# Differential attention with half of each combination on GpSimd and the turn and value product one unit later, together with six rearrangements at the joints between stages

## What is computed

```python
xn = rms_norm(x, norm_g[i]); proj = xn @ w_in[i]       # qa, ka, va, za, qb, kb, vb, zb
p1 = softmax(q1 @ k1.T * scale + t5_bias)              # differential attention, 4 heads,
p2 = softmax(q2 @ k2.T * scale + t5_bias)              # two maps of 64-wide queries and keys
oa = (p1 - lam * p2) @ va                              # values are 128 wide
ya = rms_norm(oa, subln_g[i]) * (1 - lam_init) * silu(za)
yb = neighbourhood_attention(qb, kb, vb, na_rpb[i]) * silu(zb)   # 8 heads, 8x16 windows
x = x + concat(ya, yb) @ w_out[i]
x = x + sigmoid(x @ w_ple_gate[i]) * (p[i] @ w_ple_proj[i])
```

## Time and profile before

| | us |
|---|---|
| median of 3 runs | 4010.92 |
| lowest and highest | 4009.79 to 4011.53 |
| the profiled execution | 4008.27 |
| its span, first to last instruction | 4006.5 |
| TensorE busy in the span | 3812.5 (95%) |
| VectorE, GpSimd, ScalarE busy | 2121.4, 1614.5, 1531.8 |
| mean granted TensorE clock | 0.985 |

### The profile page before, as it was taken

How to read it: one execution, slowest core, us unless ns; L and a number is a source line. 1 busy time by engine, 2 the same in 40 slices (tenths; PEclk the granted TensorE clock), 3 DMA queues, 4 the chain that set the end, 5 groups by cost and what they waited for, 6 DMA issues and landing times.

```text
span 4006.5 us, 52715 instructions
## 1 busy us (share of the span) xinstructions
PE 3812.5 (95%) x19336; PEld 3185.0 (79%) x19336; DVE 2121.4 (53%) x3622; ACT 1531.8 (38%) x2780; POOL 1614.5 (40%) x1394
## 2 busy tenths in 40 slices
PE   7999989889998999999999999897999999999999
PEld 6888777777876888778888888786888787888887
DVE  4553778523665767644454433765767643333233
ACT  4221667532334766622212122433766622222221
POOL 4242247342663610145544444563610135444442
PEclk9999999999999999999999999998999999999999
DMA  6775846320356422123233211356322131111111
GB/s 197 244 187 148 194 114 142 102 105 30 130 147 174 100 64 55 37 109 105 87 103 103 87 58 37 123 136 184 95 71 64 35 111 58 43 53 51 45 44 56
DMA packets 286153, 403.37 MB, mean 101 GB/s; under 512 B 43941, under 2 KB 206885, under 8 KB 285349
## 3 DMA queue, kind: packets, MB, share of 16 engines
q1 hardware_dynamic: 278984, 374.84, 32.7%
q10 hardware_dynamic: 6912, 25.17, 2.2%
HBM read 312.65 MB, written 96.45 MB: 102 GB/s over the span
## 4 chain that ended last, share of the span: by engine, by line
PE 71%; issue 10%; DVE 6%; POOL 5%; POOLq 2%; ACT 2%; DVEq 2%; DMA 1%; SPq 0%; ACTq 0%
PE ps L2638 6%; PE ps L2640 6%; PE ps L2639 6%; PE ps L2656 5%; PE ps L524 5%; PE ps L526 5%; PE ps L525 5%; PE ps L2658 5%; PE ps L2657 5%; PE ps L2059 3%; POOL rs L938 2%; PE ps L1705 2%; PE ps L1695 2%; PE ps L1696 2%; POOL WL L471 2%
## 5 line engine op out<-in xcount | busy, mean ns | idle before, releaser
L471 POOL TENSOR_TENSOR WL<-RAW,WH 128x1024 fp32r<-128x1024 f32 x225 | 555.5, 2480 | 752.3 <-ACT WH L445 742.2
L524 PE MATMUL ps<-WH,XTh 128*128 128x512 f32 (+1 forms) x1536 | 614.5, 400 | 38.5 <-POOL WL L471 13.6
L526 PE MATMUL ps<-WL,XTh 128*128 128x512 f32 (+1 forms) x1536 | 601.4, 392 | 0.0
L525 PE MATMUL ps<-WH,XTl 128*128 128x512 f32 (+1 forms) x1536 | 600.8, 391 | 0.0
L445 ACT ACTIVATE WH<-RAW 128x1024 fp32r<-128x1024 f32 x225 | 233.7, 1057 | 764.0 <-PE ps L2658 355.4
L2678 DVE TENSOR_TENSOR X<-ps,X 128x512 f32<-128x512 f32 x512 | 349.2, 689 | 249.5 <-PE ps L2658 248.3
L2656 PE MATMUL ps<-WH,Hh 128*128 128x512 f32 x1024 | 401.8, 392 | 4.2 <-DVE X L2678 3.9
L2669 DVE TENSOR_TENSOR MT<-ps,MT 128x512 f32<-128x512 f32 x128 | 88.5, 692 | 596.2 <-ACT MT L2692 591.2
L2638 PE MATMUL ps<-XTh,WH 128*128 128x512 f32 x1024 | 400.4, 391 | 2.3 <-ACT XTh L640 0.9
L2658 PE MATMUL ps<-WL,Hh 128*128 128x512 f32 x1024 | 399.0, 390 | 0.0
L2657 PE MATMUL ps<-WH,Hl 128*128 128x512 f32 x1024 | 398.9, 390 | 0.0
(11 more groups left out here) (274 smaller groups left out, 7770.4 us busy)
## 6 DMA issues: line engine op xcount, KB each, us to landing
RAW<-w_all SPq DMA_DIRECT2D x231, 512.0 KB, 3.6
WM<-w_mod ACTq DMA_DIRECT2D x48, 512.0 KB, 4.6
WM<-w_mod SPq DMA_DIRECT2D x48, 512.0 KB, 3.9
QKd<-KA_d SPq DMA_DIRECT2D x64, 256.0 KB, 5.8
QKm<-QM_d SPq DMA_DIRECT2D x32, 384.0 KB, 4.4
HEADK<-KA_d SPq DMA_DIRECT2D x32, 256.0 KB, 6.3
X_d<-X SPq DMA_DIRECT2D x2, 4096.0 KB, 12.6
QKd<-QA_d SPq DMA_DIRECT2D x16, 512.0 KB, 3.6
```

The source lines that it names most:

```text
L471: e.tensor_tensor(w_low(n), w_raw(n), w_high(n).bitcast(F32), ALU.subtract).then_inc(w_ready, 1)
L524: e.matmul(bank, a, w, start=(kc == 0), stop=False)
L525: e.matmul(bank, b, w, start=False, stop=False)
L526: j = e.matmul(bank, a, l, start=False, stop=(kc == K - 1))
```

## The change

In the differential attention, VectorE combines columns 0 to 511 and GpSimd columns 512 to 1023, in two operations: it scales the second map in place by the factor, then adds the first. The turn, the value product, the squares, copies, roots and output of a unit come one iteration later on their engines. TensorE's turn waits for GpSimd's part (`comb2`) after four transposes, and ScalarE's exponentials wait for it too. The loads of a head wait for the output instead of `used`, which is gone with its drain.

The six moves at joints: (1) the barrier ahead of the neighbourhood attention is gone; its first scores, maxima, exponential and three bias sums are issued inside the last iterations of the differential attention, Pn and BIn lie elsewhere, TensorE waits for the last output before it writes bank 7, and the memsets and first low values come at unit 5. (2) The PLE loads have two buffers (GT and G2) and stand, with the gate's first three weight pieces, ahead of the distance stores. (3) In the gate two squares come earlier, the highs come before the last tile's tanh and the lows in the loop. (4) The roots of the second half come between the projection's second and third weight piece. (5) A pair of "mkv" tiles shares one buffer and one store; there are three such buffers and one for "v". (6) In the dilated attention value_high(0) comes at u = 3 and the first low values at u = 4.

```diff
@@ -279,6 +278,7 @@
         c3.close()
+        PR = (GT[:], G2[:].rearrange("p a b -> p (a b)"))
         c3 = ExitStack()
...
@@ -546,7 +547,8 @@
                 if who.key == "pool":
-                    nm.roots(e, 1)
+                    if L != 1:
+                        nm.roots(e, 1)
                     if scaled(first + 3):
...
@@ -981,7 +997,7 @@
                 for k in pj.normed.get(n - 1, ()):
-                    if k in pj.vz:
+                    if k in pj.vz and pj.kinds[pj.tiles[k][0]]["half"] == 1:
                         v_store(k)
...
@@ -1083,13 +1099,13 @@
             diff_attention(who)
-            barrier(who)
             na_attention(who)
...
             distance_tables(who)
-            ple_load(who)
+            if key != "sp":
+                ple_load(who)
             gate_start(who)
...
@@ -1099,8 +1115,12 @@
                 if L == 0:
-                    if key in ("sp", "act", "pool"):
+                    if key in ("sp", "act"):
                         early(who, first, 1)
+                    if key == "pool":
+                        early(who, first, 1, 2)
+                        norm_of(1).roots(e, 1)
+                        early(who, first, 2)
                 turned = nt(who, NORM, 1 + 2 * L, X, True, first, led=norm_of(1 + 2 * L))
...
@@ -1438,9 +1458,9 @@
                     e.wait_ge(*rest_of_head(h - 1))
-                    e.wait_ge(s["used"], a.c(0) + h - 1)
+                    e.wait_ge(s["out"], a.c((h - 1) * T))
                     loads(h)
-                e.wait_ge(s["used"], a.c(0) + H_DIFF - 1)
+                e.wait_ge(s["out"], a.c((H_DIFF - 1) * T))
                 following = Heads("na", 0, 0)
...
@@ -1461,6 +1481,8 @@
                     for k in range(T):
+                        if k == T // 2:
+                            e.wait_ge(s["comb2"], a.c(u + 1))
                         j = e.transpose(ps[:, 4 + k // 4, (k % 4) * P:(k % 4) * P + P], BI[:, u % 2, k * P:k * P + P], ident[:])
...
@@ -1478,16 +1500,17 @@
                     scores(w)
-                for u in range(N + 1):
+                for u in range(N + 2):
                     if u + 2 < N:
...
                         scores(2 * u + 5)
-                    if u == N - 1:
-                        turn(u)
-                    if u >= 1:
-                        pv(u - 1)
-                    if u < N - 1:
-                        turn(u)
+                    if u == N + 1:
+                        e.wait_ge(s["max"], cm(2 * N))
+                        band_pe(who, Heads("na", 0, 0), "lead")
+                    if u >= 2:
+                        pv(u - 2)
+                    if 1 <= u <= N:
+                        turn(u - 1)
             if key == "dve":
...
@@ -1508,16 +1531,14 @@
                     e.drain()
-                    e.scalar_tensor_tensor(BI[:, u % 2, :], Pb[:, o + 1, :], li[:, u % 2:u % 2 + 1], Pb[:, o, :], ALU.mult,
-                                           ALU.add).then_inc(s["comb"], 1)
+                    e.scalar_tensor_tensor(BI[:, u % 2, 0:512], Pb[:, o + 1, 0:512], li[:, u % 2:u % 2 + 1], Pb[:, o, 0:512],
+                                           ALU.mult, ALU.add).then_inc(s["comb"], 1)
...
                                            ZS[:, home(h), t, :], ALU.mult, ALU.mult).then_inc(s["out"], 1)
-                    if t == T - 1:
-                        e.drain().then_inc(s["used"], 1)
...
@@ -1525,19 +1546,22 @@
                     e.wait_ge(v_stored(PJ["pj1"], i), 16 * T)
-                for u in range(N + 2):
+                for u in range(N + 3):
                     if u + 1 < N:
...
                         comb(u)
-                    if u >= 2:
-                        output(u - 2)
+                    if u == N + 2:
+                        band_dve(who, Heads("na", 0, 0), "lead")
+                    if u >= 3:
+                        output(u - 3)
             if key == "act":
...
                     e.wait_ge(s["comb"], a.c(u - 1))
+                    e.wait_ge(s["comb2"], a.c(u - 1))
                     o = 2 * (u % 2) + m
...
@@ -1558,16 +1582,27 @@
                 exps(1)
-                for u in range(N + 1):
+                for u in range(N + 2):
                     if u + 1 < N:
...
                         exps(2 * u + 3)
-                    if u >= 1:
-                        squares(u - 1)
-                    if u < N:
-                        copies(u)
+                    if u == N + 1:
+                        band_act(who, Heads("na", 0, 0), True)
+                    if u >= 2:
+                        squares(u - 2)
+                    if 1 <= u <= N:
+                        copies(u - 1)
             if key == "pool":
-                for u in range(N):
+                rest = slice(512, S)
+
+                def comb2(u):
+                    o = 2 * (u % 2)
+                    e.wait_ge(s["comb"], a.c(u + 1))
+                    e.tensor_scalar(Pb[:, o + 1, rest], Pb[:, o + 1, rest], li[:, u % 2:u % 2 + 1], None, ALU.mult)
+                    e.drain()
+                    e.tensor_tensor(BI[:, u % 2, rest], Pb[:, o + 1, rest], Pb[:, o, rest], ALU.add).then_inc(s["comb2"], 1)
+
+                def roots(u):
                     h, t = divmod(u, T)
...
@@ -1586,6 +1621,15 @@
+                for u in range(N + 2):
+                    if u < N:
+                        comb2(u)
+                    if u >= N:
+                        na_bias(e, u - N)
+                    if u >= 2:
+                        roots(u - 2)
+                na_bias(e, 2)
+
         def ge(e, s, value):
...
@@ -1758,10 +1802,12 @@
                     e.wait_ge(a.after.s["lo"], (a.after.L + 1) * a.after.ntr)
+                if u == 0 and a.kind == "na":
+                    e.wait_ge(AT["diff"]["out"], H_DIFF * T + CREDIT)
                 if u < N_UNITS:
...
-        def band_act(who, a):
+        def band_act(who, a, lead=False):
             e, s = who.e, a.s
...
@@ -1800,7 +1846,11 @@
-            exps(0)
+            if lead:
+                exps(0)
+                return
+            if a.kind == "dil":
+                exps(0)
             for u in range(N_UNITS + 6):
...
@@ -1808,12 +1858,12 @@
                     copy_out(u // 4 - 2)
-                if u == 1:
+                if u == (1 if a.kind == "na" else 3):
                     value_high(0)
...
-        def band_dve(who, a, part="all"):
+        def band_dve(who, a, part):
             e, s = who.e, a.s
...
@@ -1900,23 +1950,31 @@
+        def na_bias(e, u):
+            a = Heads("na", 0, 0)
+            h, t = divmod(u, T)
+            if u == 0:
+                e.wait_ge(a.s["pos"], 16)
+                e.wait_ge(*a.loaded(0))
+            e0 = (NA_START[t] - 2 * t + 8) * GRID_W
+            e.tensor_tensor(BIn[:, u % 3, :], NAB[:, h % 2, e0:e0 + NA_KEYS], RMK[:, NA_KIND[t], :], ALU.add).then_inc(a.s["bias"], 1)
+
         def na_pool(who, a):
...
                 h, t = divmod(u, T)
-                if u == 3:
+                if u == 5:
                     for t2 in range(T):
...
                     value_low(e, a, 0)
-                if t == 0:
+                if t == 0 and h:
                     e.wait_ge(*a.loaded(h))
...
                     e.wait_ge(s["max"], a.u0 + u - 2)
-                e0 = (NA_START[t] - 2 * t + 8) * GRID_W
-                e.tensor_tensor(BIn[:, u % 3, :], NAB[:, h % 2, e0:e0 + NA_KEYS], RMK[:, NA_KIND[t], :], ALU.add).then_inc(s["bias"], 1)
+                    na_bias(e, u)
                 if u % T == 7 and u + 1 < N_UNITS:
...
@@ -1938,7 +1996,7 @@
                     e.drain()
-                if u == 2:
+                if u == 4:
                     value_low(e, a, 0)
...
@@ -2203,6 +2258,8 @@
                 e.dma_start(TB[:], A["logmult"]).then_inc(s["pos"], 16)
+                ple_load(who)
+                early(who, N_IN1 + N_OUT, 0, 3)
                 for t in range(T):
...
@@ -2341,7 +2398,7 @@
             if who.key == "sp":
-                early(who, first)
+                early(who, first, 3)
             if who.key == "act":
...
@@ -2353,17 +2410,15 @@
                 for k in range(2):
-                    if k:
-                        e.wait_ge(s["add"], k)
-                    e.dma_start(PR[:], A["p_t"][k * P:k * P + P, :]).then_inc(s["ld"], 16)
+                    e.dma_start(PR[k], A["p_t"][k * P:k * P + P, :]).then_inc(s["ld"], 16)
             if key == "act":
                 for k in range(2):
-                    e.wait_ge(s["ld"], 16 * (k + 1))
-                    e.activation(PLh[:, k, :], PR[:], ACT.Copy).then_inc(s["th"], 1)
+                    e.wait_ge(s["ld"], 32)
+                    e.activation(PLh[:, k, :], PR[k], ACT.Copy).then_inc(s["th"], 1)
             if key == "pool":
...
                     e.wait_ge(s["th"], k + 1)
-                    e.tensor_tensor(PLl[:, k, :], PR[:], PLh[:, k, :].bitcast(F32), ALU.subtract).then_inc(s["add"], 1)
```

(33 more changed lines are left out.)

37 lines of the change are left out of this document (20 added, 17 removed).

## The result

The changed kernel takes **4026.0 us** (median of 5 runs, 4024.3 to 4030.3) against 4010.9 before: ratio 1.0040, 95% interval 1.0029 to 1.0052. It is slower by 0.4%, where 4000 was forecast. The profiled execution took 4030.05 us, with a span of 4028.0 us.

What follows compares the result with a forecast made beforehand. VectorE was taken to pace the differential attention, TensorE 0.3 us behind. Stage and joint +15 and other joints -26 gave -11, from the profiled 4008.3 to 3997.3 us, so a median of 4000; range 3972 to 4020.

Steps and rivals of the forecast that it cites:

- Combining on two engines: Differential attention: half the combination moves to GpSimd, which becomes the slowest engine; unit 5.5 us (5.2 to 5.75) against 4.92.
- the memsets: Joint to neighbourhood attention: GpSimd's memsets and low values hold TensorE 4.16 us; moved to unit 5, 3.5 comes back.
- Stage and joint: Differential attention and its joint to the neighbourhood attention together: +15 us (+6 at unit 5.2, +22.5 at 5.75).
- Rival 1: Differential attention: GpSimd scales at its cast's rate, unit 4.75 us, just under 4.92; kernel 3977 us; chance 0.20.
- Rival 2: Differential attention: GpSimd's turn is longer, 6.3 us, with 2 us scaling and full lock of 0.55; kernel 4024 us; chance 0.14.
- TensorE needs about 4.6 us: Differential attention: TensorE's own need per unit, taken as 0.3 us under the present 4.92 us pace.
- Gate -10: Out-product to gate: earlier loads and two buffers remove TensorE's 7.7 us wait and 2.3 us lost to the clock.
- First norm -1.5: Gate to first norm: earlier highs and roots shorten TensorE's wait of 2.83 us to about 1.5; -1.5 us (+1 to -5).
- Value stores -6: Second projection, both layers: paired stores and three pair buffers end VectorE's 6.09 us wait, TensorE's 3.00; -6 us (-4 to -10).
- Projection to dilated attention -8.5: Dilated joints: value_high(0) behind units 1 and 2 puts TensorE work ahead of its wait; 4.3 us a layer, -8.5 (-5 to -14).
- Rival 3: Gate and dilated joints: 18 us given back because the next transfers come no sooner; kernel 4009 to 4013 us; chance 0.08.

Runs made afterwards that it cites:

- experiment 5: Shared half buffers, low values early, whole combination on VectorE (3979.8 us), then 256 columns on GpSimd, or ScalarE scaling 512 or 256: 3977.4, 3980.3, 3980.9 us.
- experiment 7: Kernel before the change, with only the gate's loads changed (two PLE buffers, five loads ahead of the distance stores): 3996.2 us, ratio 0.9965.
- third kernel: Changed kernel with plain value tiles and pairs sharing four half buffers, high values back at unit 1, low values before unit 2: 4003.4 us, ratio 0.9983.

## Why the prediction was wrong, by its own steps

- **Combining on two engines: right in all terms but the memsets.** GpSimd's scaling 1.58 us (1.5), addition 1.29 (1.29), VectorE's half 0.75 (0.75), lock 0.25 (0.3), unit 5.48 (5.5). The first turn_rest of the neighbourhood attention came at 617.69 us, 20.2 later than in the earlier trace rows, of which 1.7 arose at 62 us: 18.5, as forecast. Of the memsets' 4.16 us 1.6 us came back, not 3.5. Stage and joint +16.9 against +15. Rival 1 falls with the 1.58 us, and the 384-column row was the better guide. The cast that it leaned on turned integers to float32. The same trace of before has a cast from float32 to its rounded form at less than half that pace, 1131 ns for 512 columns, which already spoke against the rival:

```profile
L1929 POOL CAST QCd<-QKd 128x512 fp32r<-128x512 f32 x32 | 35.2, 1131 | 0.0
```

The Trainium skill's "roughly line-rate" for one input (GPSIMD Engine Reference, § 4.1 Engine selection) does not hold for the scaling, by its 1.58 us for 512 columns against 1.04 for the integer cast's 1024. Rival 2 falls too; the end is close to its 4024 by coincidence, since the unit is 5.48 us and not 6.3.
- **"TensorE needs about 4.6 us" a unit: too low.** In experiment 5 TensorE is busy for 4.74 us a unit where it hardly waits. It did not matter for the forecast, because GpSimd was slower still, but it made the split look as if it could win up to 0.3 us a unit; 0.2 is nearer.
- **Gate -10: right** (-10.1 after, and in experiment 7 alone). **First norm -1.5:** +0.3 after, -3.1 to +0.1 with shared buffers and the split, -1.4 and -4.5 with the whole combination; within what differs between traces.
- **Value stores -6: the failed step.** "Three pair buffers instead of two single ones" counted what the pairs gain and never asked what the plain tiles lose: they came down from two buffers in turn to one. The tail of the projection, three plain tiles in a row with seven distance loads ahead of their stores on SP, makes that a wait of 9.66 and 9.54 us on VectorE in the two layers, and 4.8 and 4.7 us on TensorE. With all four shared and the high values' move undone (third kernel) this step does give -2.3 and -6.1 in the two layers, 8.4 against the forecast 6.
- **Projection to dilated attention -8.5: the other failed step.** I wrote that GpSimd's low values come two table steps later and may hold the first value product by a microsecond. Between unit 2 and unit 4 stand not only table steps but the casts of head 1's queries, behind a wait for that head's load. They held it 5.1 and 5.2 us in the two layers of the changed kernel, 5.0 and 7.3 with the buffers mended. With the low values left in place the move gives 7.4.
- **In both failed steps the clock was put at nothing.** The gate's term had 2.3 us for it; the terms for the stores and the dilated joints counted waits alone. The rows show 11.3 of the 14.5 us lost there as TensorE's work at a lower granted clock than before, and 3.4 as idle time.
- **Rival 3** had the right place and the wrong size: the joints did not merely give back, and the cause was not that transfers came no sooner by themselves, but that the change made them later.

In sum: -14.5 forecast for stores and dilated joints, +14.5 in the trace; these 29 us are most of the 32.8 by which the profiled execution missed its forecast (4030.1 against 3997.3). Mending both causes takes 29.9 us off the medians, more than the 26 by which the median missed 4000.

## What to carry to other kernels

When buffers are dealt out anew, count for every user how many it had and how many it has now, and look at the place where that user comes several times in a row, most often the tail of a loop: a single buffer puts each copy behind the store of the one before, and behind all that the store's queue issues first. When a step moves on an engine, list everything that stands between the old place and the new one, with its waits: a cast behind a load is worth more than the step. When a place where an engine waits is priced, look at the granted clock there too: here the lower clock took more than the added idle time. And a slow engine's whole turn, not its idle share, decides whether it can take half of an operation; before splitting one, see what waits for the slow engine's last result, and whether the next engine's pace is really shorter.

## What was not expected of the hardware

- A store of 256 KB that takes 2.5 us from issue to landing elsewhere in the projection (median of five) took 7.6 us behind seven loads of 344 KB (median 6.3 us), on top of the 2 us that it had waited to be issued.
- The lock is paid by length on both sides: the halved combination, met by the long product, took 2.60 us once and 2.1 three times in place of 0.75, so 1.4 to 1.9 us over its own time, where the whole one in the earlier trace rows took 2.2 over its own (3.47 for 1.29). Halving VectorE's operation does not halve what the lock costs. With GpSimd's product cut into eight, all 32 combinations together took 4.1 us over their shortest time, in place of 6.6.
- The same instructions, at 62 us, ran 1.4 to 1.6 us later in seven of the thirteen other kernels than in the kernel before, with the same code up to there. These seven have a granted clock of 0.66 to 0.73 from 50 to 55 us, and the other six and the kernel before have 1.00, so TensorE's clock fell there in some and not in others. What decides it is not shown. A difference of that size in one pair of traces needs a look at the clock before it is given a cause. The kernel before, then the changed one:

```profile
50.00:55.00 5.00, 3.71 (x18) 3.13 (x19) 1.47 (x3) 0.00 (x0) 4.68 (x5) 1.00 0.45 156
```

```profile
50.00:55.00 5.00, 3.65 (x13) 2.92 (x14) 1.41 (x3) 0.00 (x0) 4.71 (x4) 0.72 0.42 167
```
